# A PSUM bank for each unit's down product, a first pass written out, and gathers only for the units in use, in a mixture-of-experts kernel

## The chip, the cores and the metric

The kernel runs on one core of one Trainium2 chip. The metric is the device time of one execution in microseconds (us), lower is better. TensorE (PE in the profile) multiplies matrices, VectorE (DVE), ScalarE (ACT) and GpSimd (POOL) do the rest, and SyncE (SP) issues the large transfers.

## The reference

One layer of a transformer-like model: an adaptive norm, a gated linear recurrence beside a spatial gating unit, an output projection, and then a mixture of experts over 1,024 tokens of width 1,024. The change lies in the last part, and all that matters of it is this:

```python
top_logit, top_e = lax.top_k(logits, TOP_K)          # 4 of 32 experts for each token
gates = jax.nn.softmax(top_logit, axis=-1)
...
def expert_block(args):
    xb, e = args
    gu = xb @ w_gu[e] + b_gu[e]                       # 1024 -> 2048
    g, lin = jnp.split(gu, 2, axis=-1)
    g = jnp.minimum(g, SWIGLU_LIMIT)
    lin = jnp.clip(lin, -SWIGLU_LIMIT, SWIGLU_LIMIT)
    act = g * jax.nn.sigmoid(SWIGLU_ALPHA * g) * (lin + 1.0)
    return act @ w_down[e] + b_down[e]                # 1024 -> 1024
...
out = jnp.zeros((n_tok + 1, d)).at[row_tok].add(ys * row_gate[:, None])[:n_tok]
```

All numbers are float32. The weights of one expert are 12 MB (8 MB for `w_gu`, 4 MB for `w_down`), and all 32 experts are used.

## The kernel before

**Items and units.** The dense part takes about the first 440 us. Then the router's choice is sorted by expert, and each expert's tokens are cut into units of 32 tokens. An item is one to four units of one expert (4 x 32 = 128 rows); here there are 47 items with 143 units. Which item has how many units is known only on the chip, so every engine reads the item's words from a table (`item_value`, line 424, a load from SBUF into a register) and steps over unused units with a nest of branches: `units_down` (line 436) runs its body for u = 3, 2, 1, 0, and `by_units` (line 431) is the branch that leaves out the units that the item does not have.

**TensorE.** After the first item, whose gate and linear products are written out by hand with several list-making steps between them, each pass of the loop is `down_of(g)` and then `gate_and_linear_of(g + 1)`. `gate_and_linear(u, half)` (line 1339) multiplies a unit's rows with four chunks of `w_gu`; the result of unit u stands in PSUM bank u. `down(u)` (line 1359) multiplies the activated unit with `w_down`. In the loop its result goes to bank `4 + u % 2`, so units 3 and 1 share a bank and units 2 and 0 share the other. For u < 2 it therefore waits on `dn_drained` until VectorE has read the result that stands there. The counter `dn_drained` starts with `SPARE` = 2 already given. The last item is outside of the loop and uses `DOWN_BANK` = (4, 1, 2, 3), one bank for each unit. Around these, `make_list` (line 1299) and `repeat_rows` (line 1311) are short products that make the row lists of later items; the first waits for a one-hot matrix of VectorE, the second for VectorE's read of the list.

**VectorE.** Pass g of its loop does, in this order: read the item's words (`item_words`, three loads); `block_rows(g + 1)` (line 1942, a transpose of 128x1024), which waits for the gathered rows (`rows_in`); `make_onehot(g + 3)` (line 1934); `rows_here`, `make_idx(g + 2)` (line 1816) and `make_gates` (line 1823); `activate` for each unit (lines 1969 to 1984), which waits for the unit's gate and linear products and ends with the transpose at line 1984 that `down(u)` waits for; `read_list` (line 1802), a copy of the gates (line 2037), and `result` for each unit (lines 1991 and 1994), which reads the down product from PSUM. Before the loop its last instruction is that of line 2003.

**ScalarE.** Pass g: wait for `freed[3]`, `modulate(g + 1, 0)` (line 964, four instructions, which need `block_rows(g + 1)`), a sigmoid per unit (line 974), wait for `freed[7]`, `modulate(g + 1, 1)`. TensorE waits for these two (`z_made`) before it starts the halves of item g + 1.

**GpSimd.** Pass g: `gather(g + 2)` (line 722), four indirect transfers of 128 rows of 1 KB, one per possible unit, whether the item has it or not; they wait for `make_idx` and for `block_rows(g + 1)`. Then one scatter with addition per unit (line 733).

**SyncE.** It loads the 12 weight chunks (1 MB each) of the next expert as TensorE frees the same chunk of the last one (`freed[q]`), and the bias rows after chunk 7. SBUF holds the weights of one expert, so a chunk can only be loaded once the last item of the expert before has used it.

## Time and profile before

| what | value |
|---|---|
| time, median of 3 runs | 2048.38 us (2045.47 to 2049.39) |
| time of the profiled execution | 2049.03 us |
| its span, first to last instruction | 2047.3 us |
| mean granted TensorE clock | 0.983 |
| TensorE busy | 1940.1 us (95%) |
| VectorE busy | 989.9 us (48%) |
| ScalarE, GpSimd busy | 356.0 us (17%), 502.4 us (25%) |
| moved by DMA | 527.37 MB, mean 258 GB/s |

"Busy" is the time in which an engine has at least one instruction at work; register, branch and semaphore instructions do not count. A name such as L1359 is line 1359 of the kernel. In brackets behind an instruction of the timeline stands how long its engine was idle before it and what released it; "issue" means that the profile shows nothing that it waited for. DVEq, PEldq and SPq are the sequencers of these engines.

### The profile page before, as it was taken

How to read it: one execution, taken by the hardware profiler on the slowest of the kernel's cores; microseconds unless marked ns; L12 is line 12 of the kernel's file. 1: busy time of each engine (PE TensorE's matmuls, PEld its weight loads, DVE VectorE, ACT ScalarE, POOL GpSimd, SP SyncE). 2: the span in 40 equal slices, each digit the busy share in tenths (PEclk: the TensorE clock that was granted, in tenths of full speed). 3: DMA queues.
4: the chain of work that ended last, by engine and by line, in shares of the span. 5: the costliest groups of instructions: out<-in, count | busy, mean ns of one | idle time of the engine just before them, and what ended most of it. 6: DMA issues, size and time to landing. Idle time of an engine off the chain costs nothing.

```text
span 2047.3 us, 53441 instructions
## 1 busy us (share of the span) xinstructions
PE 1940.1 (95%) x20292; PEld 812.1 (40%) x20293; DVE 989.9 (48%) x2301; ACT 356.0 (17%) x740; POOL 502.4 (25%) x540
## 2 busy tenths in 40 slices
PE   5999989968999999999999999999999999999996
PEld 3444444523333333334343443344334443334432
DVE  4666545354534445454444444454444454444435
ACT  4243121230100101111111111111111111111003
POOL 1100022133222222323232322323223222322221
PEclk9999999989999999999999999999999999999998
DMA  9333317341871964959595979879798898999995
GB/s 375 91 136 123 123 36 215 120 180 35 292 267 26 334 225 136 381 175 367 177 364 198 387 262 370 298 287 397 278 390 290 300 390 281 393 402 346 320 340 196
DMA packets 125697, 527.37 MB, mean 258 GB/s; under 512 B 17248, under 2 KB 47600, under 8 KB 75472
## 3 DMA queue, kind: packets, MB, share of 16 engines
q1 hardware_dynamic: 92272, 470.46, 58.9%
q0 software_dynamic: 33184, 56.29, 11.8%
q8 instruction: 20, 0.33, 0.1%
q14 instruction: 29, 0.24, 0.0%
q10 hardware_dynamic: 192, 0.06, 0.0%
HBM read 494.35 MB, written 32.38 MB: 257 GB/s over the span
## 4 chain that ended last, share of the span: by engine, by line
PE 81%; DMA 10%; DVE 3%; issue 2%; ACT 1%; SPq 1%; POOL 1%; DVEq 0%; another core or an unknown queue 0%; ACTq 0%; POOLq 0%
PE psum L1339 42%; PE psum L1359 20%; PE psum L1081 8%; DMA big<-in_exp_w_down_dram 6%; PE psum L1255 5%; DMA big<-in_exp_w_gu_dram 3%; PE psum L1192 2%; PE psum L1124 1%; PE psum L1299 0%; PE psum L1096 0%; SPq L524 0%; PE psum L1311 0%; DMA big<-in_w_out_dram 0%; PE psum L1106 0%
## 5 line engine op out<-in xcount | busy, mean ns | idle before, releaser
L1339 PE MATMUL psum<-big,r 128*32 128x512 f32 x9152 | 1001.8, 596 | 17.9 <-DMA big<-in_exp_w_gu_dram 9.0
L1339 PEld LDWEIGHTS psum<-big,r 128*32 128x32 f32 x9152 | 292.9, 110 | 680.0 <-issue 657.6
L1359 PE MATMUL psum<-big,r 128*32 128x256 f32 x9152 | 519.4, 383 | 25.6 <-DVE r L1984 16.9
L733 POOL DMA_INDIRECT acc_rows<-r,scatter_idx x139 | 220.5, 1586 | 778.6 <-DVE r L1994 746.5
L1359 PEld LDWEIGHTS psum<-big,r 128*32 128x32 f32 x9152 | 303.5, 111 | 220.9 <-DVE r L1984 22.7
L964 ACT ACTIVATE r<-r,shift 128x128 f32<-128x128 f32 x368 | 150.9, 480 | 883.2 <-PE psum L1339 698.4
L1969 DVE TENSOR_TENSOR r<-psum,r 128x256 f32<-128x256 f32 x143 | 59.1, 413 | 344.8 <-PE psum L1339 258.1
L722 POOL DMA_INDIRECT r<-hs_rows,gather_idx x188 | 185.8, 988 | 83.3 <-issue 43.1
L1991 DVE TENSOR_TENSOR r<-psum,r 128x256 f32<-128x256 f32 x143 | 60.7, 425 | 272.6 <-PE psum L1359 254.7
L1081 PE MATMUL psum<-r,big 128*128 128x512 f32 x384 | 166.3, 593 | 1.6 <-ACT r L853 1.6
L1942 DVE STREAM_TRANSPOSE r<-r 128x1024 f32<-128x1024 f32 x46 | 96.0, 2087 | 105.8 <-issue 105.8
L974 ACT ACTIVATE r<-r 128x256 f32<-128x256 f32 x143 | 59.6, 417 | 465.0 <-DVE r L1975 444.0
L1255 PE MATMUL psum<-big,r 128*128 128x512 f32 x256 | 112.2, 594 | 0.7 <-DMA big<-in_w_out_dram 0.5
L1081 PEld LDWEIGHTS psum<-r,big 128*128 128x128 f32 x384 | 72.6, 190 | 91.6 <-issue 89.2
L1984 DVE STREAM_TRANSPOSE r<-r 128x256 f32<-128x256 f32 x143 | 93.3, 653 | 4.9
L1980 DVE TENSOR_TENSOR r<-r 128x256 f32<-128x256 f32 x143 | 60.9, 426 | 49.9 <-ACT r L974 49.2
L1994 DVE SCALAR_TENSOR_TENSOR r<-r,g1row,g_rows 128x256 f32<-128x256 f32 x143 | 69.3, 485 | 5.1
L1255 PEld LDWEIGHTS psum<-big,r 128*128 128x128 f32 x256 | 47.8, 190 | 59.2 <-issue 57.8
L719 POOL COPY gather_idx<-r 128x4 int32 (+1 forms) x47 | 8.7, 186 | 249.8 <-DVE r L1816 249.8
L1934 DVE TENSOR_TENSOR r<-r 128x1024 bf16<-128x1024 f32 (+1 forms) x49 | 60.0, 1226 | 7.1 <-DVE r L1932 1.5
L1982 DVE TENSOR_TENSOR r<-r 128x256 f32<-128x256 f32 x143 | 60.8, 425 | 4.9
L1971 DVE SCALAR_TENSOR_TENSOR r<-psum,r 128x256 f32<-128x256 f32 x143 | 59.3, 415 | 0.0
(316 smaller groups left out, 938.4 us busy)
## 6 DMA issues: line engine op xcount, KB each, us to landing
big<-in_exp_w_gu_dram SPq DMA_DIRECT2D x256, 1024.0 KB
big<-in_exp_w_down_dram SPq DMA_DIRECT2D x128, 1024.0 KB
big<-in_ada_w_dram SPq DMA_DIRECT2D x12, 2048.0 KB, 13.8
r<-in_x_dram SPq DMA_DIRECT2D x16, 512.0 KB, 8.7
big<-in_w_in_dram SPq DMA_DIRECT2D x4, 2048.0 KB, 19.5
r<-in_exp_b_gu_dram SPq DMA_DIRECT2D x128, 64.0 KB
big<-in_w_out_dram SPq DMA_DIRECT2D x2, 2048.0 KB, 12.7
hs_rows<-r POOLq DMA_DIRECT2D x8, 512.0 KB, 3.0
```

The costliest lines, as they stand in the source:

```text
L722: pool.indirect_dma_start(z_quarters[:, u, :], None, hs_quarters, bass.IndirectOffsetOnAxis(ap=gather_idx[:, u:u + 1], axis=0)).then_inc(r ...
L733: pool.indirect_dma_start(acc_quarters, bass.IndirectOffsetOnAxis(ap=scatter_idx[:, u:u + 1], axis=0), y_sb[:, u, :], None, bounds_check=4 ...
L964: ins_ = act.activation(izT[:, k, :].rearrange("p (u n) -> p u n", u=UMAX), z_blocks[:, :, k, :], ACT.Identity, bias=shift2[:, 1, k:k + 1] ...
L1081: last = pe.matmul(b, w[:, k, m * P:(m + 1) * P], zT[:, k, th * 512:(th + 1) * 512], start=(k == 0), stop=(k == KT - 1))
L1255: last = pe.matmul(b, src[:, ct % CT, t * P:(t + 1) * P], ring(("wout", dh))[:, ct, :], start=(ct == 0), stop=(ct == 2 * CT - 1))
L1339: last = pe.matmul(psum[32 * j:32 * j + 32, u, :].rearrange("p (a n) -> p a n", a=2), izT[:, k, u * UNIT:(u + 1) * UNIT], rhs[:, :, 256 * ...
L1359: ins_ = pe.matmul(psum[32 * i:32 * i + 32, 4 + u % 2 if bank is None else bank, 0:256], actT[:, u, f, :], down_slab(f)[:, 256 * i:256 * i ...
L1942: dve.transpose(z_blocks, z_quarters.rearrange("p u (n k) -> p u k n", k=KT)).then_inc(z_blocked, 1)
L1980: dve.tensor_tensor(gsig_sb[:, u % 2, :], gate_u, sig_sb[:, u % 2, :], ALU.mult).then_inc(gsig_made, 1)
L1982: dve.tensor_tensor(act_sb[:, u % 2, :], lin_u, gsig_sb[:, u % 2, :], ALU.mult).then_inc(act_made, 1)
L1984: dve.transpose(actT[:, u, :, :], act_sb[:, u % 2, :].rearrange("p (n k) -> p k n", k=KT)).then_inc(at_made, 1)
L1994: dve.scalar_tensor_tensor(out=y_sb[:, u, :], in0=y_sb[:, u, :], scalar=gate_cur[:, u:u + 1], in1=g2_rows[:, :], op0=ALU.mult, op1=ALU.mul ...
```

## The change

Four things are done together.

- The down product of unit u goes to bank `DOWN_BANK[u]` in all items. Banks 1, 2 and 3 are those that the same unit's gate and linear product used, which `activate` has read by then. So `down` no longer waits for results inside of an item (only u = 0 has a wait left, for the results of the item before), and the next item's `gate_and_linear(u, 0)` for u > 0 waits before its first matmul until the result of unit u has been read. The thresholds are kept in four registers, `results_of`, which `results_to_wait_for` sets in each pass. `SPARE` is 3.
- VectorE's and ScalarE's pass for item 0 is taken out of the loop and written out ahead of it. On VectorE its order is: one-hot matrix, item words, `activate` of all units, and only then `block_rows(1)`, the lists and indices, and the results. ScalarE does the sigmoids before `modulate(1, 0)`. TensorE's and GpSimd's loops keep their passes.
- GpSimd gathers only the units that the item has: one more table word is read and a nest of branches is run. The count that VectorE waits for (`rows_due`) is made by a load and a nest of branches of its own, ahead of `block_rows` in each pass.
- The number 8 of bias transfers gets a name, without effect.

```diff
@@ -68,6 +68,7 @@
...
 BIAS = 768
+BIAS_LOADS = 8
 LISTS = MAX_ITEMS + 3
...
@@ -447,7 +448,7 @@
...
-        SPARE = 2
+        SPARE = 3
         DOWN_BANK = (4, 1, 2, 3)
...
@@ -566,7 +567,7 @@
...
-                        sp_.wait_ge(bias_in, SEMW * 8 * place)
+                        sp_.wait_ge(bias_in, SEMW * BIAS_LOADS * place)
                         if place >= 2:
...
@@ -717,11 +718,18 @@
...
                 step(pool.tensor_copy(gather_idx[:, :], quarter_of[:, bass.ds(turn * UMAX, UMAX)]))
+                wanted = pool.to_reg(item_value(pool, IT_UNITS, turn, 1, UMAX))
                 pool.sem_inc(may_start, 1)
-                for u in range(UMAX):
-                    pool.indirect_dma_start(z_quarters[:, u, :], None, hs_quarters,
-                                            bass.IndirectOffsetOnAxis(ap=gather_idx[:, u:u + 1], axis=0)
-                                            ).then_inc(rows_in, SEMW)
+                units_down(pool, wanted, gather_unit)
+
+            asked = counter(pool, "asked")
+
+            def gather_unit(u):
+
+                pool.reg_add(asked, asked, SEMW)
+                pool.indirect_dma_start(z_quarters[:, u, :], None, hs_quarters,
+                                        bass.IndirectOffsetOnAxis(ap=gather_idx[:, u:u + 1], axis=0)
+                                        ).then_inc(rows_in, SEMW)
...
@@ -792,7 +800,7 @@
...
-            pool.wait_ge(rows_in, total * (UMAX * SEMW))
+            pool.wait_ge(rows_in, asked)
             pool.wait_ge(out_idx_made, 1)
...
@@ -991,8 +999,13 @@
...
             total = item_count(act)
+            units_down(act, act.to_reg(item_value(act, IT_UNITS, 0, 1, UMAX)), sigmoid)
+            act.wait_ge(freed[3], 1)
+            modulate(1, 0)
+            act.wait_ge(freed[7], 1)
+            modulate(1, 1)
             last_item = act.snap(total - 1)
-            with act.Fori(0, last_item) as g:
+            with act.Fori(1, last_item) as g:
                 units = act.to_reg(item_value(act, IT_UNITS, g, 1, UMAX))
...
@@ -1319,7 +1332,14 @@
...
             downs = counter(pe, "downs")
-            all_drained = pe.alloc_register("all_drained")
+            results_of = [counter(pe, f"results_of{u}") for u in range(UMAX)]
+
+            def results_to_wait_for():
+
+                for u in range(UMAX):
+                    pe.reg_add(results_of[u], downs, SPARE - u)
+
+            results_to_wait_for()
...
@@ -1330,11 +1350,13 @@
...
-            def gate_and_linear(u, half, first=False, between=None):
+            def gate_and_linear(u, half, first=False, between=None, steady=False):
...
                     rhs = gu_slab(k).rearrange("p (a n) -> p a n", a=2)
+                    if k == 0 and u > 0 and steady:
+                        pe.wait_ge(dn_drained, results_of[u])
                     for j in range(4):
...
@@ -1346,20 +1368,20 @@
...
-            def down(u, bank=None):
+            def down(u, last=False):
...
                 pe.wait_ge(at_made, downs)
-                if u < 2 and bank is None:
-                    pe.wait_ge(dn_drained, downs)
+                if u == 0:
+                    pe.wait_ge(dn_drained, results_of[0])
                 for f in range(KT):
...
                     for i in range(4):
-                        ins_ = pe.matmul(psum[32 * i:32 * i + 32, 4 + u % 2 if bank is None else bank, 0:256],
+                        ins_ = pe.matmul(psum[32 * i:32 * i + 32, DOWN_BANK[u], 0:256],
                                          actT[:, u, f, :], down_slab(f)[:, 256 * i:256 * i + 256],
                                          start=(f == 0), stop=(f == KT - 1), skip_group_check=True)
-                    if u == 0 and f in (1, 3, 5) and bank is None:
+                    if u == 0 and f in (1, 3, 5) and not last:
                         ins_.then_inc(freed[8 + f // 2], 1)
...
@@ -1440,7 +1462,7 @@
...
                 pe.wait_ge(z_made[0], g + 1)
-                units_down(pe, units, lambda u: gate_and_linear(u, 0))
+                units_down(pe, units, lambda u: gate_and_linear(u, 0, steady=True))
                 pe.wait_ge(z_made[1], g + 1)
...
@@ -1454,6 +1476,7 @@
...
                 begin_item()
+                results_to_wait_for()
                 gate_and_linear_of(g + 1)
...
@@ -1464,9 +1487,7 @@
...
             spread = counter(pe, "spread")
-            pe.reg_add(all_drained, downs, SPARE)
-            pe.wait_ge(dn_drained, all_drained)
-            units_down(pe, units, lambda u: down(u, DOWN_BANK[u]))
+            units_down(pe, units, lambda u: down(u, last=True))
             units_down(pe, units, spread_sum)
...
@@ -1934,9 +1955,13 @@
...
+            rows_due = counter(dve, "rows_due")
+
             def block_rows(turn):
-                dve.wait_ge(rows_in, turn * (UMAX * SEMW))
+                units_down(dve, dve.to_reg(item_value(dve, IT_UNITS, turn, 1, UMAX)),
+                           lambda u: dve.reg_add(rows_due, rows_due, SEMW))
+                dve.wait_ge(rows_in, rows_due)
                 dve.wait_ge(z_made[0], turn)
...
@@ -2013,18 +2038,31 @@
...
-                dve.wait_ge(bias_in, place * (8 * SEMW) + 8 * SEMW)
+                dve.wait_ge(bias_in, place * (BIAS_LOADS * SEMW) + BIAS_LOADS * SEMW)
                 dve.sem_inc(may_start, 1)
...
-            with dve.Fori(0, last_item) as g:
+            make_onehot(3, link)
+            units, prior, place, bias_at = item_words(0)
+            activate_all(units, place, bias_at)
+            block_rows(1)
+            rows_here(4, link)
+            make_idx(2, link)
+            make_gates(2, link)
+            read_list(5)
+            link(dve.tensor_copy(gate_cur, gate_of[:, 0:UMAX]))
+            dve.wait_ge(acc_out, prior * SEMW + SEMW * TT)
+            dve.sem_inc(may_start, 1)
+            units_down(dve, units, lambda u: result(u, bias_at, DOWN_BANK[u]))
+            base = chain[0]
+            with dve.Fori(1, last_item) as g:
                 count_ = [0]
...
                     ins_.then_inc(dve_chain, 1)
-                    dve.wait_ge(dve_chain, g * STEPS + (base + count_[0]))
+                    dve.wait_ge(dve_chain, g * STEPS + (base - STEPS + count_[0]))
...
@@ -2037,7 +2075,7 @@
...
                 dve.sem_inc(may_start, 1)
-                units_down(dve, units, lambda u: result(u, bias_at, 4 + u % 2))
+                units_down(dve, units, lambda u: result(u, bias_at, DOWN_BANK[u]))
                 assert count_[0] == STEPS
...
@@ -2047,7 +2085,7 @@
...
                 ins_.then_inc(dve_chain, 1)
-                dve.wait_ge(dve_chain, loops + (base + count_[0]))
+                dve.wait_ge(dve_chain, loops + (base - STEPS + count_[0]))
```

## Rows read from the trace of the kernel before

**Rows 1.** The page: an engine's busy time, and the group of the gathers.

```profile
PE 1940.1 (95%) x20292; PEld 812.1 (40%) x20293; DVE 989.9 (48%) x2301; ACT 356.0 (17%) x740; POOL 502.4 (25%) x540
...
L722 POOL DMA_INDIRECT r<-hs_rows,gather_idx x188 | 185.8, 988 | 83.3 <-issue 43.1
```

**Rows 2.** TensorE's waits from 508 to 2012 us: waiter, releaser, us, times, longest.

```profile
PE psum L1359 <- DVE r L1984: 11.8, 11, 4.9
PE psum L1339 <- DMA big<-in_exp_w_gu_dram: 9.0, 8, 2.7
PE psum L1359 <- DMA big<-in_exp_w_down_dram: 4.3, 6, 1.4
PE psum L1339 <- issue: 1.8, 1, 1.8
```

**Rows 3.** Timeline of TensorE through the first item's down products: start, length, instruction.

```profile
485.05 0.35 PE L1299 MATMUL psum<-g1row,r 128*128 128x6 bf16 x8 [2.01 <-DVE r L1934]
490.56 8.50 PE L1359 MATMUL psum<-big,r 128*32 128x256 f32 x128 [5.16 <-DVE r L1984]
501.10 7.11 PE L1359 MATMUL psum<-big,r 128*32 128x256 f32 x128 [2.04 <-issue]
```

**Rows 4.** Timeline of VectorE in the same stretch.

```profile
478.50 0.20 DVE L2003 TENSOR_SCALAR r<-r 128x72 f32<-128x72 f32 x1
481.22 2.07 DVE L1942 STREAM_TRANSPOSE r<-r 128x1024 f32<-128x1024 f32 x1 [2.52 <-issue]
...
483.69 1.22 DVE L1934 TENSOR_TENSOR r<-r 128x1024 bf16<-128x1024 f32 x1 [0.15 <-DVE r L1932]
...
487.44 0.42 DVE L1969 TENSOR_TENSOR r<-psum,r 128x256 f32<-128x256 f32 x1 [1.14 <-issue]
...
489.87 0.64 DVE L1984 STREAM_TRANSPOSE r<-r 128x256 f32<-128x256 f32 x1
...
498.76 0.65 DVE L1984 STREAM_TRANSPOSE r<-r 128x256 f32<-128x256 f32 x1
...
500.57 0.42 DVE L1991 TENSOR_TENSOR r<-psum,r 128x256 f32<-128x256 f32 x1 [1.05 <-issue]
```

**Rows 5.** Timeline of ScalarE in the same stretch.

```profile
483.32 1.65 ACT L964 ACTIVATE r<-r,shift 128x128 f32<-128x128 f32 x4 [23.75 <-DVE r L1942]
```

**Rows 6.** VectorE's table loads (551 to 553.7 us) and branches (486 to 487.5 us), with first and last start.

```profile
L424 DVEq TENSOR_LOAD <-r x3: 301/308/319, 551.4 to 552.9; - x3
```

```profile
L431 DVEq COMPARE_BRANCH  x3: 56/56/77, 486.5 to 487.0; - x3
```

**Rows 7.** Granted clock and DMA in two stretches: us, busy times, PEclk, DMA share, GB/s.

```profile
483.00:490.00 7.00, 0.40 (x11) 0.27 (x8) 4.78 (x17) 2.06 (x5) 2.35 (x4) 0.76 0.06 19
...
1137.00:1187.00 50.00, 46.35 (x517) 17.11 (x516) 24.66 (x63) 8.29 (x21) 13.39 (x15) 1.00 1.02 383
```

**Rows 8.** The page: the queue of GpSimd's transfers.

```profile
q0 software_dynamic: 33184, 56.29, 11.8%
```

**Rows 9.** An item of two units on VectorE, then on TensorE.

```profile
942.56 0.16 DVE L1823 TENSOR_TENSOR r<-g1row 128x4 f32 x1
945.02 0.42 DVE L1969 TENSOR_TENSOR r<-psum,r 128x256 f32<-128x256 f32 x1 [2.30 <-PE psum L1339]
```

```profile
949.41 3.29 PE L1359 MATMUL psum<-big,r 128*32 128x256 f32 x56 [0.35 <-issue]
```

**Rows 10.** An item of one unit on TensorE, and the weight wait behind it.

```profile
562.84 6.43 PE L1359 MATMUL psum<-big,r 128*32 128x256 f32 x64 [4.90 <-DVE r L1984]
571.58 1.06 PE L1339 MATMUL psum<-big,r 128*32 128x512 f32 x8 [0.27 <-DMA big<-in_exp_w_gu_dram]
574.07 1.49 PE L1339 MATMUL psum<-big,r 128*32 128x512 f32 x12 [1.43 <-DMA big<-in_exp_w_gu_dram]
```

**Rows 11.** TensorE's register work at the end of a pass, and the first matmuls behind it.

```profile
L1328 PEldq FUSED_REGOPS  x1: 74/74/74, 548.9 to 548.9; - x1
```

```profile
550.36 7.07 PE L1339 MATMUL psum<-big,r 128*32 128x512 f32 x64
```

## The prediction

> **What bounds the kernel now.** I read the page first: TensorE is busy 95% of the span, VectorE 48%, GpSimd 25% [rows 1]. So only what shortens TensorE's idle time, or what it waits for, can pay. The second view is TensorE's waits between the first and the last item: 15.1 us for weights (9.0 + 4.3, and 1.8 booked as "issue" in the middle of a weight wait) and 11.8 us for VectorE's last transpose of `activate`, of which the two items of one unit have 4.90 us each [rows 2, 10]. No row there is a wait for VectorE's read of a down product, which is what the banks are about. The third view is the timeline of the first item, which stands before that stretch and is the worst place of the expert part: TensorE waits 2.01 us for the one-hot matrix, 5.16 us for `activate` of unit 3, and 2.04 us ("issue") that end at 501.10, just when VectorE's first L1991 ends (500.57 + 0.42 = 500.99) [rows 3, 4]. That last one is the bank wait: once, not 46 times.
>
> **The first pass, step by step.** Before, VectorE is free at 478.70, reads three words, does `block_rows(1)` (2.07 us), the one-hot matrix (to 484.91) and the indices, and starts `activate` at 487.44 [rows 4]. After, the order is one-hot, words, `activate`.
> - One-hot: two table words at 0.75 us each (three loads start within 1.5 us [rows 6]) bring its first copy to 480.2; from the end of L1942 (483.29) to the end of L1934 (484.91) it took 1.6 us [rows 4], so it is done at 481.8. TensorE's list product, which started at 485.05 after waiting 2.01 us, can start at 483.05, and its wait is gone [rows 3].
> - `activate`: three words behind the start of L1934 (481.8 - 1.2 = 480.6, + 2.2 = 482.8, say 482.9), then the branches and waits ahead of L1969, 1.14 us in the row, give 484.0 where it was 487.44. From L1969 to the end of the first L1984 it is 3.07 us, so `down(3)` starts at 487.15 and not at 490.56: 3.4 us gained.
> - The 2.04 us are gone, since unit 1 has a bank of its own. TensorE's two stretches, 8.50 and 7.11 us, follow each other: 487.15 + 15.6 = 502.8, against 501.10 + 7.11 = 508.2. That is 5.4 us.
> - What is late next? The next item needs `modulate(1, 0)` and the list read. `activate` of four units takes 12.0 us (487.44 to 499.41), so it ends at 496.0. The new load and branches (1.7 us, below, 0.5 of it under the last transpose) put `block_rows(1)` at 497.2 to 499.3, ScalarE's four instructions take 1.65 us [rows 5], ready at 501.0. Lists and indices take 1.4 us, and the results start 1.05 us after the copy of the gates: result(3) is read at about 502.4. TensorE asks for it at 502.9. Nothing stops it, but by only 0.5 us.
>
> So the first pass gives 5.4 us. If the static item number makes the loads cheaper than 0.75 us, up to 6. If the list of VectorE is later than I think, the new wait takes back up to 1.5 us: the low end is 3.9. Then the clock. It was 0.76 from 483 to 490 [rows 7], so at the half level (1.2 of 2.4 GHz) for part of it, with TensorE idle 7.2 us there; the two downs behind took 8.50 us where the next two took 7.11 [rows 3]. After, it idles about 3.8 us there. If the clock stays up, 1.4 us more could come, but then result(3) at 502.4 is what it waits for, so I count 0.5 at most. Everything behind moves with it: chunks are loaded as TensorE frees them.
>
> **The gathers.** 188 gathers are issued, 4 for each of 47 turns [rows 1]; items hold 143 units, so some 45 go, on the items with one to three units, which all but a few stand between 760 and 1770 us. GpSimd's time costs nothing at 25%. What counts is the DMA engines. From 1137 to 1187 us they are at a share of 1.02 and move 383 GB/s [rows 7], and in that stretch stand four waits of TensorE for weights. One gather is 0.131 MB. At 383 GB/s it is 0.34 us; by its queue's share, 11.8% of 2047.3 us for 56.29 MB [rows 8], 0.56 us. In each of three such stretches (near 1187, 1267 and 1453 us) three gathers go, 1.0 to 1.7 us each time, of waits of 4.0, 3.4 and 1.7 us. Two smaller waits (0.18 and 0.45 us) can vanish too. Sum: 3.6 to 5.7 us. The load wait ends with the last chunk, and not all saved bytes stand ahead of it, so I take 4.0. The low end is nothing (the transfers run between the chunks in idle slots), the high end 6.
>
> **The price on VectorE.** Each pass now has a load (0.75 us) and three branches (0.25 us apart [rows 6]) with up to four register adds ahead of `block_rows`: 1.6 to 1.9 us, in the same chain that ends in `activate`. In items with three or four units there are several us between the chain's end and the first products. In an item of two units the chain ends at 942.72, 1.14 us of branches bring it to 943.9, and `activate` starts at 945.02: 1.1 us of cover [rows 9]. So it starts 0.5 to 0.8 us late. TensorE then has a hole of its own right behind (0.35 us idle, and 56 of 64 matmuls only from 949.41), which swallows most of it; I count 1.0 us over the eleven such items, and 0 to 7 as bounds. In the two items of one unit there is no cover: TensorE waits 4.90 us and would wait 6.6. But behind both it waits for weights, 1.7 us at 571 to 574 us [rows 10] and 2.7 us at the second, which came from chunks freed before; so that is free, and costs 3.4 us if that cover is gone.
>
> The Trainium skill ("Advanced Engine Details and Errata", section Control Flow Timing) gives 108 ns for a compare-and-branch; the record here shows 56 ns, but one every 0.25 us, so the trace's spacing is used. By the page the sum on VectorE would be 0.4 us less per pass.
>
> **The price on TensorE.** Four register adds per pass and a wait ahead of units 3 to 1. The register work of `begin_item` runs at 548.9, the first matmul behind it at 550.36 [rows 11]: its sequencer is about a microsecond ahead even with the branches, and four adds need 0.2 to 0.4. Nothing. Unit u's result is read some 5 us after the gate products end, the next item's first matmul comes 7 to 14 us after: no wait either. The wait of `down` in later items cost nothing, so its going gives nothing. ScalarE's order matters in the first pass alone; SP's wait has the same meaning. GpSimd's second gather comes 13 us later, ahead of the first scatters, and both are waited for only at about 508 and 536 us.
>
> **Sum.** -5.4 - 4.0 + 1.0 = -8.4 us. Against the profiled execution's 2049.03 this is 2040.6; that execution is 0.65 us above the median of the runs shown, so I say 2040.5.
>
> **Rivals.**
> - *Only the first pass pays* (the gathers were hidden in the DMA's idle slots). For it: they are 5% of the bytes. Against it: a DMA share of 1.02 in those stretches. 2049.0 - 5.4 + 1.0 = 2044.6, or 2043 to 2046.
> - *More comes than I count*: the full 6 us from gathers, no loss on VectorE, and TensorE's clock stays up in the first pass and behind the 2.7 us wait near 1267 us: -6 - 6 - 1.5 = 2035.5.
> - *The control work takes TensorE's place in the queue* (slower). Its sequencer leads by about 1 us; if adds and waits took more than that, each of 46 passes would pay the excess. It decides at 9.4 / 46 = 0.2 us a pass; 0.5 us would be +23 - 9.4, 2062. The same sign comes if VectorE's 1.7 us are not covered in the eleven items of two units: 11 x 1.7 = 19 us, 2058. Against both stand the leads above.
> - *A jump over unused units costs more than before.* The hole ahead of 949.41 stands behind a jump over the bodies of two units [rows 9]. It costs about 0.8 us in an item of two units; if the longer loops made such a hole in every pass, 46 x 0.8 = 37 us, less 9.4, give 2076. The Trainium skill ("Runtime: NRT & Kernel Launch", section Instruction fetch mechanics) says that a taken branch whose target is outside of the loaded window stalls for a fetch of its page; by that rule the new branches speak against the change. The rows fit with it in items of two units only.
>
> **How the numbers follow.** My forecast 0.50 (2037.5 to 2043), only the first pass 0.22, more than counted 0.12, control work 0.11, jumps 0.05. The range is 2034.5 to 2046.5: it leaves out the slow cases and the tail of the third. A measurement of this kernel tells about 0.2% (4 us) from nothing, so "faster" ends at 2044.3: 0.50 + 0.12 and half of 0.22 make 0.73; the other half and a little of the fourth are "same", 0.14; "slower" is 0.13.
>
> **What would show it.** In the profile after: the first L1359 at about 487, L1311 at about 502.8, no 2.04 us wait, one-hot ahead of 483; about 143 gathers; the waits for weights near 1187, 1267 and 1453 us smaller by 1 to 1.7 us each; VectorE's L1942 1.7 us later behind the last result; the one-unit items' 4.90 us grown to 6.6 and the weight waits behind them shrunk. The prediction is wrong if L1339 sits idle behind L1991, if holes stand between L1311 and L1339 in each pass, or if TensorE's waits for L1984 grow past 20 us between 508 and 2012 us.

## The result, and the profile after

| | before | after |
|---|---|---|
| median of 4 runs each | 2046.93 us (2045.25 to 2049.39) | 2030.18 us (2029.01 to 2032.85) |
| profiled execution, its span | 2049.03, 2047.3 us | 2029.01, 2027.2 us |
| mean granted TensorE clock | 0.983 | 0.985 |

The ratio is 0.9923, 95% interval 0.9907 to 0.9939: 15.8 us faster, or 12.5 to 19. The forecast of 2040.5 us had the sign right and half of the size; its range ended at 2034.5, so the time lies outside of it. One execution of a kernel below, the banks alone, took 7784.52 us at a granted clock of 0.466 and is left out of every figure.

The page after, with the lines that answer to [rows 1, 8] (some lines of the program moved: the gate product is now L1361, the down product L1381, the gather L730):

```profile
PE 1927.8 (95%) x20292; PEld 799.9 (39%) x20293; DVE 991.5 (49%) x2301; ACT 356.0 (18%) x740; POOL 461.3 (23%) x495
...
q0 software_dynamic: 31024, 50.39, 11.1%
q8 instruction: 20, 0.33, 0.1%
q14 instruction: 30, 0.25, 0.0%
...
L730 POOL DMA_INDIRECT r<-hs_rows,gather_idx x143 | 143.0, 1000 | 123.1 <-issue 123.1
```

So 45 gathers and 5.90 MB went, as foreseen. TensorE's timeline of the first item, after, against [rows 3]:

```profile
484.39 0.35 PE L1312 MATMUL psum<-g1row,r 128*128 128x6 bf16 x8
488.05 15.62 PE L1381 MATMUL psum<-big,r 128*32 128x256 f32 x256 [3.30 <-DVE r L2009]
503.60 0.25 PE L1324 MATMUL psum<-g1row,r 128*128 128x6 bf16 x4
503.78 16.52 PE L1361 MATMUL psum<-big,r 128*32 128x512 f32 x152
```

And VectorE's, against [rows 4]:

```profile
481.94 1.22 DVE L1955 TENSOR_TENSOR r<-r 128x1024 bf16<-128x1024 f32 x1
484.93 0.42 DVE L1994 TENSOR_TENSOR r<-psum,r 128x256 f32<-128x256 f32 x1 [1.77 <-PE psum L1420]
...
497.95 2.13 DVE L1967 STREAM_TRANSPOSE r<-r 128x1024 f32<-128x1024 f32 x1 [0.96 <-issue]
...
502.52 0.42 DVE L2016 TENSOR_TENSOR r<-psum,r 128x256 f32<-128x256 f32 x1 [1.06 <-issue]
```

The 2.01 us wait for the one-hot matrix is gone, the 5.16 us became 3.30, and the four down products run in one piece. The first gate product of the expert part stood at 445.32 us before and at 446.86 after (the dense part differs by that much between executions), so 1.54 us are to be taken off each start above. In these terms the second item starts at 502.24 us where it started at 508.33: 6.1 us earlier.

The waits of TensorE in the body of the expert part, after, from 520 to 1990 us:

```profile
PE psum L1381 <- DVE r L2009: 9.8, 2, 4.9
PE psum L1361 <- DMA big<-in_exp_w_gu_dram: 8.3, 7, 1.8
PE psum L1381 <- DMA big<-in_exp_w_down_dram: 5.8, 6, 1.4
PE psum L1312 <- DVE r L1955: 3.3, 2, 1.7
```

Beside [rows 2] this looks as if nothing had been won at the weights: 14.1 us of waits now, 15.1 then. Yet from the start of the second item to the end of the last down product it took 1502.3 us and before 1517.9. The first puzzle was thus where 15.6 us of the body had been, in a trace that shows no such wait.

### The profile page after: what moved, and what is told of

It reads as the page before. It is cut to its first block, busy times and chain, and to the rows that moved or that the text cites. A ratio compares the mean times of both kernels' runs of the same rounds, so it can differ in the third digit from the quotient of the medians.

```text
span 2027.2 us, 54425 instructions
## 1 busy us (share of the span) xinstructions
PE 1927.8 (95%) x20292; PEld 799.9 (39%) x20293; DVE 991.5 (49%) x2301; ACT 356.0 (18%) x740; POOL 461.3 (23%) x495
## 3 DMA queue, kind: packets, MB, share of 16 engines
q0 software_dynamic: 31024, 50.39, 11.1%
## 4 chain that ended last, share of the span: by engine, by line
PE 83%; DMA 11%; DVE 2%; ACT 1%; issue 1%; SPq 1%; POOL 1%; DVEq 0%; ACTq 0%; POOLq 0%
PE psum L1361 41%; PE psum L1381 22%; PE psum L1094 8%; DMA big<-in_exp_w_down_dram 7%; PE psum L1268 5%; DMA big<-in_exp_w_gu_dram 3%; PE psum L1205 2%; PE psum L1137 1%; PE psum L1312 1%; ACT r L844 0%; DMA big<-in_w_out_dram 0%; PE psum L1324 0%; SPq L525 0%; PE psum L1119 0%; PE psum L1223 0%
## 5 line engine op out<-in xcount | busy, mean ns | idle before, releaser
L1361 PE MATMUL psum<-big,r 128*32 128x512 f32 x9152 | 997.8, 594 | 15.5 <-DMA big<-in_exp_w_gu_dram 8.3
L1361 PEld LDWEIGHTS psum<-big,r 128*32 128x32 f32 x9152 | 291.7, 110 | 674.7 <-issue 652.7
L1381 PE MATMUL psum<-big,r 128*32 128x256 f32 x9152 | 509.9, 382 | 18.9 <-DVE r L2009 13.1
L1381 PEld LDWEIGHTS psum<-big,r 128*32 128x32 f32 x9152 | 292.8, 111 | 215.5 <-DVE r L2009 13.3
L730 POOL DMA_INDIRECT r<-hs_rows,gather_idx x143 | 143.0, 1000 | 123.1 <-issue 123.1
```

The costliest lines, as they stand in the source:

```text
L730: pool.indirect_dma_start(z_quarters[:, u, :], None, hs_quarters, bass.IndirectOffsetOnAxis(ap=gather_idx[:, u:u + 1], axis=0)).then_inc(r ...
L1361: last = pe.matmul(psum[32 * j:32 * j + 32, u, :].rearrange("p (a n) -> p a n", a=2), izT[:, k, u * UNIT:(u + 1) * UNIT], rhs[:, :, 256 * ...
L1381: ins_ = pe.matmul(psum[32 * i:32 * i + 32, DOWN_BANK[u], 0:256], actT[:, u, f, :], down_slab(f)[:, 256 * i:256 * i + 256], start=(f == 0) ...
```

## The experiments

Twelve kernels ran, in three groups, each group on one chip with runs of the kernel before beside them. "Lead-in" is the time from the first gate product to the first one of the second item; "body" is from there to the end of the last down product, both from TensorE's timeline of the profiled execution. Behind the last down product come 20.3 to 21.5 us in every kernel. "Weight waits" is the time that TensorE waited for DMA of `in_exp_w_gu` and `in_exp_w_down` from 520 to 1990 us; what is booked as "issue" is left out. The difference is the ratio's distance from 1 times 2045 us.

| kernel | ratio, 95% interval | difference, us | lead-in | body | weight waits |
|---|---|---|---|---|---|
| before, first trace | | | 63.0 | 1517.9 | 13.3 |
| before, run again | 1.0003 (0.9994 to 1.0012) | +0.6 | 62.9 | 1512.8 | 25.4 |
| banks | 0.9996 (0.9982 to 1.0011) | -0.8 | 60.5 | 1516.7 | 25.0 |
| first pass | 1.0013 (1.0001 to 1.0025) | +2.7 | 64.3 | 1511.1 | 20.9 |
| gathers | 0.9963 (0.9947 to 0.9980) | -7.6 | 64.9 | 1505.2 | 12.5 |
| VectorE's count alone | 1.0005 (0.9996 to 1.0014) | +1.0 | 64.7 | 1509.6 | 20.4 |
| banks + first pass | 0.9975 (0.9964 to 0.9986) | -5.1 | 57.5 | 1511.0 | 20.7 |
| banks + gathers | 0.9948 (0.9934 to 0.9961) | -10.6 | 63.3 | 1504.2 | 14.8 |
| first pass + gathers | 0.9967 (0.9956 to 0.9979) | -6.7 | 66.5 | 1505.3 | 13.9 |
| the whole change | 0.9923 (0.9907 to 0.9939) | -15.8 | 56.9 | 1502.3 | 14.1 |
| whole, old wait back | 0.9925 (0.9903 to 0.9948) | -15.3 | 57.4 | 1502.2 | 12.7 |
| whole, cheap count | 0.9920 (0.9905 to 0.9934) | -16.4 | 57.4 | 1502.6 | 14.8 |
| whole, 94 short gathers more | 0.9960 (0.9946 to 0.9974) | -8.2 | 57.3 | 1508.9 | 17.9 |
| whole, 94 gathers more | 1.0015 (1.0001 to 1.0028) | +3.1 | 57.1 | 1521.3 | 26.5 |

**The banks alone.** The down product of unit u in bank `DOWN_BANK[u]`, with the waits that belong to it; order of passes and gathers as before.

```diff
-        SPARE = 2
+        SPARE = 3
...
-                if u < 2 and bank is None:
-                    pe.wait_ge(dn_drained, downs)
+                if u == 0:
+                    pe.wait_ge(dn_drained, results_of[0])
...
+                    if k == 0 and u > 0 and steady:
+                        pe.wait_ge(dn_drained, results_of[u])
```

> The banks and their waits alone, with the first pass and the gathers as before. The trace of the changed kernel shows the down products of the items of two units in 7.11 us where they took 8.0 to 8.4, twelve times, some 12 us that the prediction did not have. Theory W (the extra wait ahead of down(1), or the shared bank, makes TensorE's hole): the two-unit items fall to 7.1 us here too, the 2.04 us of the first item go, and the time is 13 to 15 us below the kernel before. Theory V (VectorE's later arrival in these items takes the hole away): the hole stays, and only about 2 us are gained.

Measured 2044.1 against 2044.91 us. TensorE's timeline of its first item:

```profile
486.86 0.35 PE L1299 MATMUL psum<-g1row,r 128*128 128x6 bf16 x8 [1.78 <-DVE r L1942]
492.37 15.48 PE L1368 MATMUL psum<-big,r 128*32 128x256 f32 x256 [5.16 <-DVE r L1992]
```

The wait between unit 2 and unit 1 is gone here and the two in front of it have stayed: the lead-in is 2.5 us shorter in the trace, where 2.04 us were foretold, and over the whole kernel that is not to be told from nothing. The two-unit items (eleven of them, not twelve) have no holes and take 7.1 us, as theory W had it; but its 13 to 15 us did not come, so neither theory fits.

**The first pass alone.** VectorE's and ScalarE's pass 0 written out in the new order, with `4 + u % 2` as bank, so that `down(1)` still waits for result(3).

```diff
+            make_onehot(3, link)
+            units, prior, place, bias_at = item_words(0)
+            activate_all(units, place, bias_at)
+            block_rows(1)
...
+            units_down(dve, units, lambda u: result(u, bias_at, 4 + u % 2))
```

> The first pass written out on VectorE and ScalarE alone, with two shared banks and all gathers. VectorE reads the first results only after block_rows, lists and indices, and down(1) waits for result(3): by my working result(3) is read at about 502, so down(1) starts there where it started at 501.1, and the pass gains nothing: 0 to 2 us slower in the first item, 0 in the rest. If the parts were independent it would gain 3.4 us. The two-unit items should keep 8.0 to 8.4 us under both theories W and V.

Measured 2047.26 us, ratio 1.0013, 2.7 us slower (0.2 to 5.1). Its TensorE timeline:

```profile
488.37 8.80 PE L1364 MATMUL psum<-big,r 128*32 128x256 f32 x128 [3.23 <-DVE r L1989]
502.14 8.80 PE L1364 MATMUL psum<-big,r 128*32 128x256 f32 x128 [4.96 <-issue]
```

The down products start as early as in the whole change, but the results are now read behind `block_rows` and the lists, and the third product waits 4.96 us for the bank. The new order is worth something only with banks of their own. The items of two units take 7.1 us here too, though TensorE's program is that of before; both theories had them at 8.0 to 8.4 us.

**The gathers alone.** GpSimd asks only for the units in use, and VectorE counts them; nothing else.

```diff
+                wanted = pool.to_reg(item_value(pool, IT_UNITS, turn, 1, UMAX))
...
+                units_down(pool, wanted, gather_unit)
...
+                units_down(dve, dve.to_reg(item_value(dve, IT_UNITS, turn, 1, UMAX)),
+                           lambda u: dve.reg_add(rows_due, rows_due, SEMW))
+                dve.wait_ge(rows_in, rows_due)
```

> The gathers only for units in use, with VectorE's extra load and branches in each pass, banks and first pass as before. Predicted: 3 us gained (4.0 from fewer bytes in DMA-bound stretches, 1.0 lost on VectorE). Theory W: the two-unit items keep their 8.0 to 8.4 us. Theory V: they fall to 7.1 us here, and 12 us more are gained, 15 in all.

Measured 2039.18 us: 7.6 us faster (4.1 to 10.8), although the lead-in became 1.9 us longer. For this part alone I had expected 3 us, so it brings two and a half times as much. The items of two units take 7.1 us, as theory V had it, but its 15 us are outside of the interval.

**The whole change, with a wait that is always met put back** ahead of `down(1)`:

```diff
-                if u == 0:
+                if u < 2:
                     pe.wait_ge(dn_drained, results_of[0])
```

> The changed kernel with one wait put back: ahead of the down product of unit 1, on the results of the item before, which are long read, so it never has to hold anything up. If the wait itself (one more semaphore in the wait ahead of down(1)) makes the hole, the two-unit items return to 8.0 to 8.4 us and the time rises by about 12 us. If it is the shared bank or VectorE's timing, they stay at 7.1 us and the time is that of the changed kernel.

2030.52 us, the same as the whole change. So the wait ahead of `down(1)` is not what made the holes (the items of two units stay at 7.1 us), and what pays is not that it went from TensorE's queue.

**The kernel before once more**, for a second trace of the same program.

> The kernel before, unchanged, with a trace of its own. The holes in its twelve items of two units (down products 8.0 to 8.4 us where 7.11 would do) were gone in all of the first three experiments, the one that left TensorE's program as it was among them. If the holes belong to the program, they are here again. If they belong to that one execution, the down products of these items take 7.1 us here, and the span from the second item's start to the last down product is within 3 us of the 1517.9 of the first trace, since the transfers set the pace there.

The time is the same (1.0003), the trace is not: the body is 5.1 us shorter, where at most 3 were expected. TensorE's waits from 520 to 1990 us:

```profile
PE psum L1339 <- DMA big<-in_exp_w_gu_dram: 14.6, 10, 2.6
PE psum L1359 <- DMA big<-in_exp_w_down_dram: 10.8, 11, 1.4
PE psum L1359 <- DVE r L1984: 9.8, 2, 4.9
PE psum L1339 <- issue: 0.5, 2, 0.3
```

There are 25.4 us of weight waits where the first trace had 13.3. What that one had in their place is seen in the groups by line of the same stretch. The first trace:

```profile
L1359 PE MATMUL psum<-big,r 128*32 128x256 f32 x8640 | 489.8, 383 | 18.4 <-DVE r L1984 11.8 <-DMA big<-in_exp_w_down_dram 4.3 <-issue 1.8
```

The second trace of the same kernel:

```profile
L1359 PE MATMUL psum<-big,r 128*32 128x256 f32 x8640 | 480.8, 381 | 20.7 <-DMA big<-in_exp_w_down_dram 10.8 <-DVE r L1984 9.8
```

The same 8640 products took 9 us more in the first. Of these, 2.6 us stand in the two items of one unit (6.43 and 6.18 us against 4.93 and 5.11); the granted clock from 560 to 570 us was 0.66 in the first trace and 0.83 in the second. The others go with the holes at the start of down products that the prediction had found in items of two units [rows 9]: all eleven took 8.0 to 8.4 us, 11.5 us too many in all, some of it booked as idle. The second trace has the same item without one:

```profile
945.17 0.35 PE L1299 MATMUL psum<-g1row,r 128*128 128x6 bf16 x8
945.45 7.11 PE L1359 MATMUL psum<-big,r 128*32 128x256 f32 x128
```

None of the other thirteen traces has these holes, and four of them besides this one are of kernels that leave TensorE's program as it was. They belonged to one execution and not to the program. That in this one execution TensorE came later to its next weights, and so waited less for them, is argued and not tried. The figures fit: the holes (+11.5 us), the slower matmuls in the two items of one unit and behind the 2.7 us wait near 1267 us (+2.6 and +1.7) and the smaller weight waits (-10.3, with what is booked as "issue") come to 5.5 us, and the body is 5.1 us longer.

**Banks and first pass together**, with all gathers; the two diffs above put together, with `DOWN_BANK[u]` in both.

> Banks and first pass together, gathers as before. Theory P (the two need each other: alone the banks gave 2.5 us of the first item and the first pass took 1.3): the first item's down products end 5.4 to 6 us earlier, nothing else changes, and the time is 6 us below the kernel before, 2039. Rival: the parts simply add up from their single times, 0 and +2 us, and nothing is gained here.

2039.39 us, 5.1 us faster, and the lead-in is 57.5 us: all that the first item gives comes from this pair, and it takes both.

**VectorE's count alone.** The load and the branches ahead of `block_rows`, but the wait and all gathers as before:

```diff
+                units_down(dve, dve.to_reg(item_value(dve, IT_UNITS, turn, 1, UMAX)),
+                           lambda u: dve.reg_add(rows_due, rows_due, SEMW))
                 dve.wait_ge(rows_in, turn * (UMAX * SEMW))
```

> The kernel before with the extra load, branches and register adds of VectorE in each pass, but every gather is still made and waited for as before. The prediction put this at 1 us, with 0 to 7 as bounds, plus 1.6 us in the first item, which has no cover in this order of the first pass. So 1 to 3 us slower than before. If the control work is what changes TensorE's pace (theory V), the time falls by several us instead.

2046.54 us, +1.0, with an interval that includes no difference at all. The lead-in grew by 1.9 us, the body did not grow. What the count costs, it costs in the first item, where the chain over VectorE sets TensorE's start; the order of the written-out pass takes it off that chain again.

**Banks and gathers**, without the first pass.

> Banks and gathers together, first pass as before. Theory G (TensorE's pace from 1137 to 1763 us is set by the transfers as a whole, so each gather that goes is worth its transfer time there, and banks add only the 2.0 us of the first item): 7.6 us from the gathers alone plus 2, 9 to 10 us below the kernel before, some 6 above the full change. Theory C (the banks are worth more once the transfers are lighter): 12 us or more below it.

2035.41 us, 10.6 us faster (8.0 to 13.5): theory G's 9 to 10 is the nearer one, and theory C's 12 or more is not excluded by the time. The body, 1504.2 us, is that of the gathers alone less 1.0, so the traces give no sign of theory C.

**First pass and gathers**, with the shared banks.

> The written-out first pass and the gathers for the units in use, with the shared banks and waits of before. Theory A (the parts add, but the first pass needs the banks): the gathers give the 8 us that they gave alone, the first pass by itself gives nothing, because unit 1's down product then waits for a result that VectorE reads late: about 2038.5 us, 7 to 8 below before, and from the first gate product to the second item's about 64 us, where the full change has 57. Rival B (the parts need one another in other ways: the first pass pays once the gathers are fewer): below 2034 us.

2039.25 us (6.7 faster), the lead-in 66.5 us. Its timeline shows the wait of the first pass alone, 1.1 us longer; VectorE's count stands ahead of its results too:

```profile
505.31 9.96 PE L1371 MATMUL psum<-big,r 128*32 128x256 f32 x128 [6.08 <-issue]
```

So theory A holds: the gathers give theirs, and the first pass without banks nothing.

**More gathers.** To the whole change come two gathers per item, in all 47 items, into memory that nobody reads, with VectorE waiting for them too:

```diff
                 units_down(pool, wanted, gather_unit)
+                pool.reg_add(asked, asked, 2 * SEMW)
+                for b in range(2):
+                    pool.indirect_dma_start(more[:, b, :], None, hs_rows.rearrange("r (i n) -> (r i) n", i=4),
+                                            bass.IndirectOffsetOnAxis(ap=gather_idx[:, b:b + 1], axis=0)
+                                            ).then_inc(rows_in, SEMW)
...
+                dve.reg_add(rows_due, rows_due, 2 * SEMW)
```

> The changed kernel with two gathers more for each item, in all items, of 128 rows of 1 KB each (0.131 MB), into memory that nobody reads: 94 more or nearly, 12 MB. It does more than the change wants and computes the same. Theory A (every gather takes its transfer time from a stream of weights that bounds the stretch, 0.17 to 0.19 us each, as the 45 did that went away): 2030.5 + 16 to 18, about 2047 us. Rival B (only those gathers cost that stand in items of one to three units, where the weights are late; in items of four units, about half of them, they lie in idle slots of the DMA engines): 2030.5 + 4 to 9, 2035 to 2039 us. Rival C (what the gathers cost is not the transfer but something else that went with them): no change.

2048.05 us. Against the whole change (0.9923; with the cheap count, on this chip, 0.9920) the ratio is larger by 0.0092, 18.8 us, and the body by 19.0 us: 0.20 us for each of 94 gathers. The page and the waits (520 to 1990 us) of this kernel:

```profile
q0 software_dynamic: 35536, 62.71, 12.4%
...
L727 POOL DMA_INDIRECT r<-hs_rows,gather_idx x94 | 90.6, 964 | 28.6 <-issue 28.6
```

```profile
PE psum L1387 <- DMA big<-in_exp_w_down_dram: 13.8, 14, 1.4
PE psum L1367 <- DMA big<-in_exp_w_gu_dram: 12.7, 11, 1.6
PE psum L1387 <- DVE r L2016: 9.8, 2, 4.9
```

The weight waits are up from 14.1 to 26.5 us, and VectorE's 9.8 us did not move. Rival B, by which the gathers of full items are free, had 4 to 9 us and is out, also when it is counted afresh: the full items are 17 of 47 and not half, so it should have had 60 gathers of 0.17 to 0.19 us, 10 to 11 us, where the intervals of the two ratios together leave 14.5 or more. Theory A stands, a little above its 16 to 18. Not all of the 19.0 us is waiting: TensorE's idle time from 520 to 1990 us is up by 12.6 us. The other 6.4 us are then longer matmuls, 3.1 us of them in the down product (483.4 against 480.3); behind two waits for weights near 1443 us, for instance, 144 of them took 9.66 us, with a granted clock of 0.83 from 1440 to 1450 us, where 7.98 is usual.

**More gathers, short ones.** The same with rows of 256 bytes:

```diff
-                    pool.indirect_dma_start(more[:, b, :], None, hs_rows.rearrange("r (i n) -> (r i) n", i=4),
+                    pool.indirect_dma_start(more[:, b, :], None, hs_rows.rearrange("r (i n) -> (r i) n", i=16),
```

> As the kernel with two gathers more for each item, but each of the 128 rows is 256 bytes long and not 1 KB: as many transfers, a quarter of their bytes. Theory A (the bytes are what costs): a quarter of what the two more gathers cost, 1 to 4.5 us above the changed kernel. Rival B (each row costs by its being there, whatever its length): as much as with rows of 1 KB. Rival C (neither costs): no change.

2037.49 us. By the ratios that is 7.6 us above the whole change, by the body 6.6 us; 3.08 MB more instead of 12.32. Theory A's 1 to 4.5 us were too few, rival B's full price is out. Between the two kernels stand 9.24 MB and 12.4 us of body, 1.34 us for a megabyte, or 0.18 us for a gather's 0.131 MB. Then the 12.32 MB would be 16.5 us, and 2.5 us of the 19 would be independent of the bytes (3.9 us of 18.8 by the ratios). Each ratio has an interval of 2.7 to 2.9 us to either side, so that most of the cost is bytes is shown, and the size of the rest is not.

**A cheaper count.** The whole change, but VectorE adds units times 16 instead of branching:

```diff
-                units_down(dve, dve.to_reg(item_value(dve, IT_UNITS, turn, 1, UMAX)),
-                           lambda u: dve.reg_add(rows_due, rows_due, SEMW))
+                dve.reg_mul(more_rows, dve.to_reg(item_value(dve, IT_UNITS, turn, 1, UMAX)), SEMW)
+                dve.reg_add(rows_due, rows_due, more_rows)
```

> The changed kernel with VectorE's count of the rows to come made without branches: the item's number of units times 16 is added to the count, so three branches and up to four additions a pass become one product and one addition. Theory A (VectorE's control work is covered in all items but those of one unit, and there a wait for weights behind it takes it up): the time of the changed kernel within 1 us, 2029.5 to 2031, though VectorE's transpose at the head of each pass comes 0.75 us or more earlier. Rival B (the control work costs TensorE time in the items of one and two units, 0.8 us each of 13): 3 to 10 us faster, 2020 to 2027.

2029.11 us, nominally the best of all and not to be told from the whole change (the intervals lie over one another). The time alone does not exclude the low end of rival B, 3 us; the body, 1502.6 us where it was 1502.3, speaks for theory A. VectorE's groups of the transpose at the head of a pass, 520 to 1990 us, before:

```profile
L1942 DVE STREAM_TRANSPOSE r<-r 128x1024 f32<-128x1024 f32 x44 | 91.9, 2088 | 100.9 <-issue 100.9
```

after:

```profile
L1967 DVE STREAM_TRANSPOSE r<-r 128x1024 f32<-128x1024 f32 x44 | 91.8, 2087 | 166.6 <-issue 166.6
```

and with the cheaper count:

```profile
L1968 DVE STREAM_TRANSPOSE r<-r 128x1024 f32<-128x1024 f32 x44 | 91.8, 2086 | 137.9 <-issue 137.9
```

The idle time ahead of each transpose is 2.29, 3.79 and 3.13 us. The count costs 1.50 us a pass, and a product and an addition in place of its branches and additions take 0.65 off; that brings TensorE nothing that can be measured.

## Why the prediction was wrong

**The first pass: right.** -5.4 us was forecast, the lead-in of the trace is 6.1 us shorter, and the pair that makes it measured -5.1 by itself. Step by step, with the 1.54 us taken off: one-hot done at 481.6 (481.8 forecast), `activate` at 483.4 (484.0), `down(3)` at 486.5 (487.15), four down products in 15.62 us (15.6), their end at 502.1 (502.8), result(3) read at 501.4 (502.4). The wait of the next item for it did not come; it had 0.8 us to spare where 0.5 was forecast. The granted clock over that idle stretch was 0.76 before [rows 7] and, with the 1.54 us added (484.5 to 491.5 us), 0.76 after too; the four down products took 15.6 us in both, so the 0.5 us at most that I gave to the clock is not seen.

**The gathers: the term that was mis-sized.** The mechanism was right, the size was half. The step that failed reads "of waits of 4.0, 3.4 and 1.7 us ... Sum: 3.6 to 5.7 us", cut to 4.0 with 6 as the upper end. Both come from the weight waits that one trace showed, 15.1 us in all: three gathers in each of three stretches, nine of the 45, and two smaller waits, were taken for all there was to win. Measured: 7.6 us by the kernel with the gathers alone, 8.6 us between the mean bodies of the five traces of the table with all gathers (1512.2, the first trace left out) and of the six with fewer (1503.6), and 0.20 us each when 94 are added. The weight waits say the same: they are 20.4 to 25.4 us, 22.5 in the mean, in those five, and 12.5 to 14.8, 13.8 in the mean, in those six, 8.7 us less. A better clock is not what the six have: one minus the granted clock, added up in steps of 10 us from 510 to 2000 us, comes to 7.5 us in the mean of the five and 8.0 in that of the six. At 0.17 to 0.20 us each, 45 gathers are 7.6 to 9 us (the 7.6 us are net of what VectorE's count costs); the forecast's 4.0 was 0.09 us each. The rival that had more coming, 6 us of it from gathers, was capped by the same waits.

Where the waits went is seen in the second trace of before beside that after. TensorE's timeline from 1130 to 1480 us, before:

```profile
1157.56 10.51 PE L1339 MATMUL psum<-big,r 128*32 128x512 f32 x96 [1.45 <-DMA big<-in_exp_w_gu_dram]
1170.71 7.93 PE L1339 MATMUL psum<-big,r 128*32 128x512 f32 x72 [2.65 <-DMA big<-in_exp_w_gu_dram]
...
1360.20 7.98 PE L1359 MATMUL psum<-big,r 128*32 128x256 f32 x144 [1.36 <-DMA big<-in_exp_w_down_dram]
```

After:

```profile
1150.81 10.51 PE L1361 MATMUL psum<-big,r 128*32 128x512 f32 x96 [1.36 <-DMA big<-in_exp_w_gu_dram]
1163.10 7.93 PE L1361 MATMUL psum<-big,r 128*32 128x512 f32 x72 [1.78 <-DMA big<-in_exp_w_gu_dram]
```

The same waits, smaller by 0.1 and 0.9 us, and the one at 1360 us gone. Of the three stretches that I foresaw, with 1.0 to 1.7 us each, the one near 1187 us (1157 to 1183 in this trace) gives 1.1 us in all, that near 1267 us 0.3 and that near 1453 us 0.5; the one near 1360 us, where the first trace shows no wait for weights, gives 1.7. So one came as foreseen, and the others give a little or stand elsewhere. The whole body's weight waits fall from 25.4 to 14.1 us between these two traces, more than between the two groups of traces.

**The holes: read as a property of the program.** "TensorE then has a hole of its own right behind, ... which swallows most of it", and with it the rival of the jumps. The second trace has no holes, the traces of the changed kernel have none, and that rival falls. The Trainium skill ("Runtime: NRT & Kernel Launch", section Instruction fetch mechanics) has a taken branch stall where its target is outside of the loaded window. No run here shows such a stall: the two instruction queues on the profile's page moved 20 and 29 packets in the execution with the holes and 20 and 29 in the second one of the same kernel, which has none; in the changed kernel they are 20 and 30. The holes did more harm elsewhere: the trace on which the gathers were sized has some 10 us less of weight waits than the second one. What [rows 2] shows was a true reading of an untypical execution.

**VectorE's count: the duration about right, the place wrong.** 1.6 to 1.9 us a pass ahead of the transpose were forecast; 1.50 us is what the groups show. The +1.0 us was put on the eleven items of two units; these take 7.1 us with no wait for VectorE, with and without the count. Where it stands alone it measured +1.0 as well, but that is luck: its lead-in grew by 1.9 us and its body did not grow. In the whole change it costs nothing that can be seen: with 0.65 us less of it a pass no difference in time can be told. The item of one unit shows why. Its timeline in the second trace of before:

```profile
562.91 4.93 PE L1359 MATMUL psum<-big,r 128*32 128x256 f32 x64 [4.92 <-DVE r L1984]
...
570.88 1.07 PE L1339 MATMUL psum<-big,r 128*32 128x512 f32 x8 [0.99 <-DMA big<-in_exp_w_gu_dram]
573.38 7.07 PE L1339 MATMUL psum<-big,r 128*32 128x512 f32 x64 [1.43 <-DMA big<-in_exp_w_gu_dram]
```

After:

```profile
554.56 0.35 PE L1312 MATMUL psum<-g1row,r 128*128 128x6 bf16 x8 [1.68 <-DVE r L1955]
559.80 5.22 PE L1381 MATMUL psum<-big,r 128*32 128x256 f32 x64 [4.88 <-DVE r L2009]
...
568.69 11.80 PE L1361 MATMUL psum<-big,r 128*32 128x512 f32 x108 [0.77 <-DMA big<-in_exp_w_gu_dram]
```

The delay is there, 1.68 us, but ahead of the list product and not in the 4.90 us as forecast; and behind it the waits for weights are 0.77 us where they were 2.42. The two cancel, as the prediction had it. The second item of this kind does the same: 1.64 us ahead of the list product, 4.89 us where it was 4.91, and waits for weights of 0.38 us where they were 2.40.

**TensorE's control: right.** The old wait put back costs nothing. The four additions and the new waits come with the banks: the body with banks and first pass (1511.0) lies among those without banks (1509.6 to 1512.8), and with fewer gathers it is 1504.2 with banks and 1505.2 without. Only the trace of the banks alone has a longer one, 1516.7, and its median time is not longer than that of before. Some 3.4 us of this are seen: in two items of three units, near 1450 and 1715 us, 144 matmuls of the down product took 9.66 us where the second trace of before has 7.98, with a granted clock of 0.91 over 20 us (1440 to 1460, 1705 to 1725) where that one has 1.00. A fall of the clock behind a wait for weights is no matter of the banks: the first trace of before has it too (0.91 and 0.92 from 1260 to 1280 us, behind the 2.7 us wait).

**The sum by the measured terms.** The pair of banks and first pass gives 5.1 us and the gathers 7.6, together 12.7; the whole change gave 15.8 (12.5 to 19), 15.3 and, with the cheap count, 16.4. About 3 us more than the two parts thus remain. Of these the traces account for 1.9: the kernel with the gathers alone pays VectorE's count in its lead-in (64.9 and not 63.0), and the whole change does not. The last 1 us lies inside of the intervals. The forecast also started high: 8.4 us off the 2048.38 us that it had as the median would be 2040.0, and the runs of before beside the change had a median of 2046.93.

**Open.** What made the holes in the one execution was not found: they did not come again, so nothing could be tried on them. That it was not more instruction packets is all that the traces show.

## What to carry to other kernels

Before a term is capped by the waits that a trace shows, take a second trace of the same program: two executions here, 5 us apart in span, had 13.3 and 25.4 us of waits for the same transfers. Five traces with all gathers, the untypical one not among them, still spread from 20.4 to 25.4. Where a stream of loads is late in many places by a little, what is taken from the DMA engines is worth its price per transfer times the number of transfers, not just what stands beside the largest waits; adding the suspect, in a known dose, gives that price directly (here within about a quarter). And parts of a change may need one another: the new order alone made the kernel no faster, the banks alone hardly, and both together 5 us.

## What the runs showed of the hardware

- The down product's 8640 matmuls took 489.8 us in one execution and 480.3 to 485.9 us in the thirteen others, with a granted clock of 1.00 from 940 to 960 us, where one of the holes is; in that item the idle time is booked as "issue" (0.35 us) and as a wait for VectorE (0.18 us), and the rest as busy.
- Behind the same idle stretch of 4.9 us the 64 matmuls of the first one-unit item's down product took 6.43 us in one execution of the kernel before and 4.93 us in another; the granted clock from 560 to 570 us was 0.66 and 0.83.
- One gather of 128 rows of 1 KB costs this kernel 0.20 us when it is added, and 0.17 to 0.19 us when it is taken away, though 0.131 MB at the 383 GB/s of the stretch in [rows 7] would be 0.34 us: 0.5 to 0.6 of its bytes' time reaches TensorE. With rows of a quarter of the length it costs 0.07 to 0.08 us and not 0.05.
- A gather of 128 rows is 48 packets in its queue ((33184 - 31024) / 45), and with rows of 256 bytes 32.
- VectorE's load of a table word with three branches and up to four additions takes 1.50 us a pass in the whole change and 1.30 us where only the count is added; a product and an addition in place of the branches and additions take 0.65 us less.
